# SBUF tensors placed at multiples of 128 bytes, and repeated semaphore waits left out

## What is computed

```python
def reference(x, mem, positions, g_mix, w_in, ...):
    x = first_block(...)      # h = rms_norm(x); q,k,v,z,xbc,dt = h @ w_in; dilated attention and an SSD mixer;
                              # x += [attn, ssm] @ w_out; x += cross_attention(x, mem);
                              # x += square(relu(rms_norm(x) @ w_up)) @ w_down
    return second_block(x, ...)  # h = x @ w_in_2; LRU recurrence and top-k attention, gated, @ w_out_2; layer_norm;
                                 # x @ w_up_2, causal convolution, silu(gate) * up, @ w_down_2; layer_norm
```

## The kernel before

| tensor | address before | mod 128 | address after | mod 128 |
|---|---|---|---|---|
| cst | 16512 | 0 | 146560 | 0 |
| cols | 23200 | 32 | 153248 | 32 |
| xT | 26208 | 96 | 102528 | 0 |
| raw | 42592 | 96 | 82048 | 0 |
| WH | 63072 | 96 | 16512 | 0 |
| WL | 79456 | 96 | 32896 | 0 |
| XH | 95840 | 96 | 49280 | 0 |
| XL | 112224 | 96 | 65664 | 0 |
| small, rb | 128608, 129632 | 96 | 145536, 141440 | 0 |
| P0-P2, T0-T7 | from 133888 | 0 | from 118912 | 0 |
| AH2, AL2, AH4, AL4 (`AH`, `AL`), MH, ML, qT and the rest of the stages | from 156416 | 0 | the same | 0 |

## Time and profile before

### The profile page before, as it was taken

One profiled execution on the slowest core, in us unless ns is written; L12 is line 12 of the kernel. 1 busy time (PEld: TensorE's weight loads), 2 busy tenths in 40 slices (PEclk: granted clock), 3 DMA queues, 4 the chain that ended last, 5 costly groups with the idle time before them and its releaser, 6 DMA issues.

```text
span 2835.7 us, 53264 instructions
## 1 busy us (share of the span) xinstructions
PE 2782.2 (98%) x22440; PEld 2721.1 (96%) x22440; DVE 1789.4 (63%) x2601; ACT 1340.8 (47%) x1811; POOL 112.2 (4%) x75
## 2 busy tenths in 40 slices
PE   8999999999999999999999999999899999999997
PEld 8998889899999999999899999999899999999997
DVE  6787679575555555555576786455576646654666
ACT  5464566454344343444344774444354434443543
POOL 2000021010000000000000000000400000000003
PEclk9999999999999999999999999999899999999998
DMA  6544445465555555555454555555365555555552
GB/s 237 170 133 136 156 142 179 134 196 186 186 184 186 186 185 187 182 186 170 148 157 146 168 172 185 183 183 163 119 194 185 184 187 182 185 186 186 181 184 89
DMA packets 136606, 488.49 MB, mean 172 GB/s; under 512 B 15152, under 2 KB 17584, under 8 KB 136368
## 3 DMA queue, kind: packets, MB, share of 16 engines
q1 hardware_dynamic: 136368, 485.09, 53.1%
HBM read 482.93 MB, written 2.10 MB: 171 GB/s over the span
## 4 chain that ended last, share of the span: by engine, by line
PE 97%; DVE 2%; ACT 1%; DMA 0%; issue 0%; SPq 0%; ACTq 0%; DVEq 0%
PE ps L727 95%; PE ps L730 1%; DVE T L1664 1%; DMA cst<-in_cst 0%; ACT xT L1150 0%; DVE small L1672 0%; DVE WL L1664 0%; DVE q L1664 0%; DVE XL L1664 0%; ACT P L1150 0%; DVE small L1664 0%; ACT T L1150 0%; DVE P L1668 0%; SPq L685 0%; SPq L682 0%
## 5 line engine op out<-in xcount | busy, mean ns | idle before, releaser
L1664 DVE TENSOR_TENSOR WL<-raw,WH 128x1024 fp32r<-128x1024 f32 x907 | 1120.7, 1238 | 864.5 <-ACT WH L1150 861.6
L1150 ACT ACTIVATE WH<-raw 128x1024 fp32r<-128x1024 f32 x907 | 960.5, 1059 | 1425.0 <-PE ps L727 1421.6
L727 PE MATMUL ps<-XH,WH 128*128 128x256 f32 x5024 | 1437.9, 286 | 22.0 <-issue 9.7
L727 PE MATMUL ps<-XL,WH 128*128 128x256 f32 x5024 | 1424.5, 284 | 0.0
L727 PE MATMUL ps<-XH,WL 128*128 128x256 f32 x5024 | 1424.3, 283 | 0.0
L727 PEld LDWEIGHTS ps<-XH,WH 128*128 128x128 f32 x5024 | 964.6, 192 | 30.1 <-issue 25.6
L727 PEld LDWEIGHTS ps<-XL,WH 128*128 128x128 f32 x5024 | 964.7, 192 | 2.3 <-issue 1.5
L727 PEld LDWEIGHTS ps<-XH,WL 128*128 128x128 f32 x5024 | 964.3, 192 | 0.3
L727 PE MATMUL ps<-AH,WH 128*128 128x256 f32 x1856 | 520.7, 281 | 0.3 <-DVE AL L1664 0.3
L727 PE MATMUL ps<-AL,WH 128*128 128x256 f32 x1856 | 519.9, 280 | 0.0
L727 PE MATMUL ps<-AH,WL 128*128 128x256 f32 x1856 | 519.8, 280 | 0.0
(11 more groups left out here) (227 smaller groups left out, 1642.0 us busy)
## 6 DMA issues: line engine op xcount, KB each, us to landing
raw<-in_w_up SPq DMA_DIRECT2D x304, 512.0 KB, 3.5
raw<-in_w_in SPq DMA_DIRECT2D x224, 512.0 KB, 3.5
raw<-in_w_down SPq DMA_DIRECT2D x216, 512.0 KB, 3.4
raw<-in_w_out SPq DMA_DIRECT2D x64, 512.0 KB, 3.4
raw<-in_w_gates SPq DMA_DIRECT2D x64, 512.0 KB, 3.5
raw<-in_w_ckv SPq DMA_DIRECT2D x16, 512.0 KB, 3.7
raw<-in_w_cq SPq DMA_DIRECT2D x8, 512.0 KB, 3.9
raw<-in_w_co SPq DMA_DIRECT2D x8, 512.0 KB, 3.3
```

Source lines behind the costliest of these rows:

```text
L727: return e.matmul(out, l, r, start=start, stop=True, skip_group_check=True)
L1150: return e.activation(out, x, func, **kw)
L1664: return e.tensor_tensor(out, a, b, op)
```

## The change

The calls of `sb` are put in another order, so that the large tensors come first and begin at multiples of 128 bytes. A class `Waits` remembers for each engine the highest value that it has waited for on each semaphore, and leaves out a wait that is already satisfied by an earlier one; all `e.wait_ge(...)` become `on.wait_ge(...)`.

```diff
+class Waits:
+    def __init__(self, e):
+        self.e, self.seen = e, {}
+
+    def wait_ge(self, sem, value):
+        if self.seen.get(sem.name, 0) < value:
+            self.seen[sem.name] = value
+            self.e.wait_ge(sem, value)
...
-        cst = sb("cst", [128, CN])
-        cols = sb("cols", [128, VN])
-        xT = sb("xT", [128, 16, 256])
-        raw = sb("raw", [128, RAW, GRAN])
         WH = sb("WH", [128, RING, GRAN], F32R)
         WL = sb("WL", [128, RING, GRAN], F32R)
         XH = sb("XH", [128, 16, 256], F32R)
         XL = sb("XL", [128, 16, 256], F32R)
+        raw = sb("raw", [128, RAW, GRAN])
+        xT = sb("xT", [128, 16, 256])
+        Ps = [sb(f"P{i}", [128, 512]) for i in range(NP)]
+        Ts = [sb(f"T{i}", [128, 512]) for i in range(NT)]
+        rb = sb("rb", [128, 4, 256])
         small = sb("small", [128, 256])
-        rb = sb("rb", [128, 4, 256])
+        cst = sb("cst", [128, CN])
+        cols = sb("cols", [128, VN])
         rcol = sb("rcol", [128, 16])
         stat = sb("stat", [128, 24])
-        Ps = [sb(f"P{i}", [128, 512]) for i in range(NP)]
-        Ts = [sb(f"T{i}", [128, 512]) for i in range(NT)]
...
         def tensor(e):
+            on = Waits(e)
...
-                e.wait_ge(s["lo"], g + 1)
+                on.wait_ge(s["lo"], g + 1)
```

More of the change, by code:

```diff
@@ L719, in sync @@
                     if l == 1:
-                        e.wait_ge(*s("ln_gain", 8 + u + 1))
+                        on.wait_ge(*s("ln_gain", 8 + u + 1))
                         e.dma_start(A["out"][:, 2 * u:2 * u + 2, :], xT[:, 2 * u:2 * u + 2, :]).then_inc(s["out"], 16)
-            e.wait_ge(s["out"], 128)
+            on.wait_ge(s["out"], 128)
         def tensor(e):
+            on = Waits(e)
             def mm(out, l, r, start=True):
@@ L1297, in ca_hi @@
             def ca_hi(u):
-                e.wait_ge(s["gemm"], P.count("v", 1) if u < 4 else P.count("w_out_a", 3))
-                e.wait_ge(*s("adda", u + 1))
+                on.wait_ge(s["gemm"], P.count("v", 1) if u < 4 else P.count("w_out_a", 3))
+                on.wait_ge(*s("adda", u + 1))
                 gain_high(XH, (2 * u + 8) % 16, xT, "g_cross", 2 * u)
@@ L1324, in up_relu @@
             def up_relu(u):
-                free_T(e, "up", u)
-                e.wait_ge(s["gemm"], P.count("w_up", u // 2))
+                free_T(on, "up", u)
+                on.wait_ge(s["gemm"], P.count("w_up", u // 2))
                 fn(T("up", u)[:, :], bank("w_up", u // 2, u % 2)[:, :], ACT.Relu).then_inc(s["up_relu"], 1)
@@ L1736, in norm_rs @@
                     m.then_inc(*own.up())
-                    e.wait_ge(*own.now)
+                    on.wait_ge(*own.now)
                     m = tt(col, col, col, ALU.mult)
@@ L1862, in rope_angle @@
                 a = T("rope")[:, 0:256]
-                free_T(e, "rope")
-                e.wait_ge(s["pos"], 16)
+                free_T(on, "rope")
+                on.wait_ge(s["pos"], 16)
                 e.tensor_copy(a, cosA[:, :].bitcast(I32)).then_inc(*own.up())
-                e.wait_ge(*own.now)
+                on.wait_ge(*own.now)
                 ts(a, a, C("invf"), None, ALU.mult).then_inc(s["rope_angle"], 1)
@@ L1949, in sm_norm @@
                 p, m, blocks = Pt("sm", H), sm_root(H), head(H)[3]
-                e.wait_ge(*s("sm_exp", H + 1))
+                on.wait_ge(*s("sm_exp", H + 1))
                 e.reciprocal(m[:, 6:8], m[:, 4:6]).then_inc(*own.up())
-                e.wait_ge(*own.now)
+                on.wait_ge(*own.now)
                 a = 0
@@ L2041, in lam_x @@
             def lam_x(_):
-                e.wait_ge(*s("mem_lo", 8))
+                on.wait_ge(*s("mem_lo", 8))
                 ts(sps[:, 0, :], V("lru_lam", 0, 16), -1.0, None, ALU.mult).then_inc(*own.up())
-                e.wait_ge(*own.now)
+                on.wait_ge(*own.now)
                 softplus_start(sps[:, 0, :], sps[:, 1, :], sps[:, 2, :]).then_inc(s["lam_x"], 1)
             def lam_one(_):
-                e.wait_ge(*s("lam_exp", 1))
+                on.wait_ge(*s("lam_exp", 1))
@@ L2088, in tk_start @@
             def tk_start(_):
-                e.wait_ge(*s("ix_acc", 16))
+                on.wait_ge(*s("ix_acc", 16))
                 tt(score[:, :], score[:, :], C("causal"), ALU.add).then_inc(*own.up())
-                e.wait_ge(*own.now)
+                on.wait_ge(*own.now)
                 e.tensor_copy(work[:, :], score[:, :]).then_inc(s["tk_start"], 1)
             def tk_round(i):
-                e.wait_ge(*(s("tk_round", i) if i else s("tk_start", 1)))
+                on.wait_ge(*(s("tk_round", i) if i else s("tk_start", 1)))
                 for t, (a, b) in enumerate(rows):
@@ L2120, in rq @@
                 tt(to, y, twice(tab[:, 0, :]), ALU.mult).then_inc(*own.up())
-                e.wait_ge(*own.now)
+                on.wait_ge(*own.now)
                 tt(to[0:64, :, :], to[0:64, :, :], b[0:64, :, :], ALU.add).then_inc(s["rq"], 1)
             def xr_taps(u):
-                e.wait_ge(*s("xr_tap", u + 1))
+                on.wait_ge(*s("xr_tap", u + 1))
                 taps = [[V("rnn_w", w * 16 + 2 * u + k) for w in range(4)] for k in range(2)]
@@ L2160, in gr_poly @@
                 b = T("gr", u)[:, :]
-                e.wait_ge(*s("gr_sq", u + 1))
+                on.wait_ge(*s("gr_sq", u + 1))
                 ts(b, b, 0.044715, 1.0, ALU.mult, ALU.add).then_inc(*own.up())
-                e.wait_ge(*own.now)
+                on.wait_ge(*own.now)
                 tt(b, b, bank("gr", u // 2, u % 2)[:, :], ALU.mult).then_inc(s["gr_poly"], 1)
```

668 lines of the change are left out of this document (334 added, 334 removed).

## The result

The changed kernel takes 2847.52 us (median of 6 runs, 2846.22 to 2849.66) beside 2837.01 us for the kernel before: a ratio of 1.0035, 95% interval [1.0024, 1.0046]. It is 0.35% **slower**, a small loss that the interval keeps clear of noise, where 2716 us was forecast.

The account below looks back on a forecast made before the run. TensorE's matmul stream was taken as the bound, through the distance between matmul starts. From the profiled execution, 2837.5 - 126.9 (addresses) + 6 (stalls) = 2716.6, with the median 0.5 lower: 2716 us, range 2670 to 2806 us.

Parts of the forecast that it names:

- What bounds the kernel: Whole kernel: TensorE's matmul stream, busy 98% of the span; time is the sum of distances between matmul starts.
- My reading: Matmul stream: one 6.67 ns slot per 64-byte piece touched, plus one for the stationary load, 1.6 to 2 if offsets differ.
- 99.9 us on X: Saving on 14,976 matmuls with moving XH/XL, as in w_up: from 120.0 to 113.3 ns each.
- rival 3: No difference: XH's unchanged 32,768-byte distance behind WH holds X at 120.0 ns, A gains little; 2837 us, chance 0.08.
- 23.8 us on A and M: Saving on 5952 matmuls with moving AH/AL or MH/ML, as in w_down: 4.0 ns each.
- 3.2 us on 512 columns: Saving on matmuls with 512 moving columns, as in v and w_cv: 1.9 us and 1.3 us.
- rival 4: Slower: equal operand offsets lock the reads at the slow rate, X stays, A rises to 120.0 ns; 2853 us, chance 0.06.
- Rival 1: Only the moving operand's alignment counts: X drops to A's rate, saving 40 us, A stays; 2797 us, chance 0.20.
- Rival 2: The stationary load is the floor: distances fall to 112.5 or 109.1 ns; 2700 or 2629 us, chance 0.18.
- The 109.2 ns for an isolated gap: Skill page's formula N / 2.4 + 2.5 ns for 256 columns; its sum would be the lower end of rival 2.
- Waits, VectorE, ScalarE, DMA at nothing: Removed waits and the operands moved on the other engines and loads: priced at 0; TensorE gain between 0 and 9.7 us.
- The 6 us given back: TensorE idle slices between 200 and 600 us, 5.6 us in all, expected to double under a faster stream: +6 us.

Follow-up runs that it names:

- e8: Changed kernel with pads: WL 128 bytes, XH, XL, A and M 192 bytes (modulo 256) from WH; 2724.67 us, 0.9600 of the kernel before.
- m1: Matmuls-only program, 96 per block, sweeping operand address offsets, both tensors of a kind together; 120.00 ns per matmul at difference 0, 113.33 at 192.
- m2: Matmuls-only program, differences in 8-byte steps and WL, XH, XL shifted separately in 64 combinations; no block below 113.33 ns, three combinations there.
- e2: Changed kernel with the old SBUF order, so only the repeated waits are left out; 2838.54 us, 1.0003 of the kernel before.
- e4: Changed kernel with pads putting XH, XL and all A and M tensors 192 bytes (modulo 256) from WH and WL; 2772.33 us, ratio 0.977.

## Why the prediction was wrong

- **What bounds the kernel**: right. In every kernel here the time followed the distance between matmul starts, and in e8 a stream at 113.3 ns still left TensorE busy for 98% of the span.
- **The step that failed** is "My reading: a moving operand costs one slot for each 64-byte piece that it touches, and a load of 128 stationary columns beside it costs one more slot if both begin at the same offset in a piece". `dt` did not move when its operand was aligned, and `w_up` stands at 120.0 ns with everything aligned, not at 113.3. m1 shows what sets the rate instead: the difference of the two operands' addresses, while a common shift did nothing. I had compared operands by their own remainders and so saw two variables where one, their difference, gives the four distances with 128 stationary columns: 120.0 (`X`, 0), 117.3 (`A`, 160), 233.3 (`w_cv`, moving `WH` at -160, which is 96; m1 gives 233.33 at 352, the same modulo 256), 226.7 (`v`, 0; m1 226.67). The fifth, `dt`, stays open (last section). One of the five was also a favourable stretch: over the whole of job `v` the distances below 245 ns have a mean of 229.7 ns, in `w_cv` 233.3, so the 6.7 ns between them that I built on are 3.6 on average.
- **99.9 us on X**: measured 0. `XH` moved together with `WH`. This is what rival 3 named as its condition ("`XH` lies exactly 32,768 bytes behind `WH` before and after. If that distance and not the remainder holds the pair at 120.0, `X` stays").
- **23.8 us on A and M**: measured -7.8 us, a loss, because their difference went from 160 to 128.
- **3.2 us on 512 columns**: measured 0. `v`, `w_cv` and `v2` together take 123.6 us before and after; the difference stays 0 in `v` and `v2`, and in `w_cv` it went from 96 to 128, which m1 and m2 have at 233.3 and 232.3 ns.
- **Rivals.** Rival 3 had `X` right and `A` wrong; rival 4 the direction and the place, "`w_down` after the change is above 117.3 ns", but its mechanism, equality of remainders, is not the cause: at m1's difference 64 remainders modulo 64 are equal too, and it runs at 117.78 ns. It gave `A` 120.0 ns where 118.6 was measured. Together they had 0.14; they deserved more, because the reading rested on no row with both operands aligned and rival 3 needed only the layout's arithmetic. Rival 1 falls because `X` did not drop to the rate of `A`. Rival 2 named distances of 112.5 and 109.1 ns, and no block of m1 or m2 with 128 stationary columns came below 113.33.
- **Against the Trainium skill.** I set aside the second, independent read port of the Trainium skill, "TensorE: Matmul & The Clock Gate", section "Step-by-step: what each phase is for", on `v` against `w_cv`. The runs agree with setting it aside: in m1 the relative address of the two streams alone moved the distance between 113.33 and 123.33 ns, so they are not independent here. The 109.2 ns for an isolated gap at 256 columns, by the formula of the Trainium skill, same page, section "Back-to-back issue gap", appeared in no block; the lowest is 113.33.
- **Waits, VectorE, ScalarE, DMA at nothing**: right. e2 measured 1.0003, and VectorE's 1788.4 us of busy time after the change lie beside 1789.4 us.
- **The 6 us given back**: too much. In e8, where the stream did get to 113.3 ns, TensorE's idle time in the three stretches of the earlier trace rows is 1.05 + 1.42 + 4.44 = 6.9 us instead of 5.6:
```profile
200.00:300.00 100.00, 98.95 (x684) 86.36 (x684) 73.52 (x191) 46.77 (x79) 0.00 (x0) 1.00 0.42 139
400.00:500.00 100.00, 98.58 (x862) 97.81 (x861) 85.74 (x152) 56.15 (x82) 13.88 (x10) 1.00 0.55 178
500.00:600.00 100.00, 95.56 (x679) 88.27 (x678) 70.27 (x121) 52.08 (x85) 10.50 (x8) 0.97 0.50 163
```
  What e8 lacks against the sum is elsewhere, added up from job start to job start in the profiled executions: `X` saved 90.2 of the 99.9 us, `A` and `M` 22.5 of 23.8, and the 512-column jobs lost 1.5 us instead of gaining 3.2. `X` falls short in the jobs that small steps interrupt: `q2` and `xr` saved 8.3 us of 10.2, while `rnn` and `att`, uninterrupted, saved all that was priced.
- The price of the rate itself was nearly right: e8, with its long streams at 113.3 ns, takes 2724.67 us. The change does not bring them there.

## What to carry to other kernels

Before pricing an alignment, write down the addresses of both operands that are read at the same time and take their difference as well as each remainder; a change that moves both together may change nothing. Where the whole kernel is one stream of matmuls, a small program that sweeps the offset in blocks of 96 matmuls settles in one run what stretches of a real kernel only hint at. A good offset should be timed several times in the full kernel, since one set of offsets can hold two rates, and the small program can show the one and the full kernel the other.

## What the runs showed of the hardware

- The distance between starts of matmuls on `F32R` operands with a new 128-column stationary operand each and 256 moving columns lies between 113.33 and 123.33 ns at a clock of 1.00, by the relative SBUF addresses of the operands (m1, m2). Where the high and low tensors lie alike it follows the difference modulo 256 bytes, with exceptions (672 against 160; 80 in m1 against m2). A common shift had no effect at differences 0 and 128 (m1).
- With 512 moving columns the same difference matters: 226.67 ns at 0, 228.9 at 64, 232.3 to 234.3 ns at 32, 96, 128, 160, 192 and 224. With 16 stationary columns m1 and m2 show 113.33 ns at some differences (96, 128, 192, 224, 256) and 116.67 at others (0, 64, 160), so 0 and 256 differ here and 256 bytes is not the period. In `dt` the stationary pieces lie 64 bytes apart, so its difference walks through 0, 192, 128 and 64, before and after alike; it runs at 113.3 in both kernels, and what sets that stays open.
- At a difference of 192 two steady rates exist, 113.3 and 117.8 ns, and an execution can keep the slower one through all rounds of `w_up` and `w_down` (e4). With `WL` shifted by another 128 bytes the long jobs of the profiled execution have only the faster one, and all four executions lie within 5.3 us (e8). Why 192 and 112 are good, and what holds a rate, was not settled.
- Repeated waits that are already satisfied cost nothing measurable: 127 fewer wait instructions on TensorE and 274 fewer on ScalarE changed the time by a ratio of 1.0003 [0.9994, 1.0012].
